# A fused two-layer block on one core: how each later stage begins, and who transposes x for it

## The chip, the core and the metric

One core of a Trainium2 chip runs the whole program in one launch. The time is the device time of one execution in microseconds; the median of three runs stands for the kernel. TensorE multiplies, VectorE and ScalarE prepare its operands and take its results away, GpSimd does a few small elementwise operations, and SyncE issues the weight loads.

## The reference, cut to what matters

x is 256 tokens by 2048 features, float32. Five stages follow one another, each a chain of large products with weights that are read once:

```
for layer in 0, 1:
    h = rms_norm(x, mix_pre_g[layer])
    m = pool_conformer_mixer(h, ...) if layer == 0 else short_conv_mixer(h, ...)
    x = x + rms_norm(m, mix_post_g[layer])
    h = rms_norm(x, ffn_pre_g[layer])
    x = x + rms_norm(relu(h @ w1) ** 2 @ w2, ffn_post_g[layer])
h = rms_norm(x, norm_g_2)
proj = h @ w_in          # q, k, v, z_a, u_b, v_b, z_b, g_a, g_b
x = x + (sigmoid(g_a) * y_a + sigmoid(g_b) * y_b) @ w_out
```

The stages are numbered 0 (mixer of layer 0), 1 (its feed-forward part), 2 (mixer of layer 1), 3 (its feed-forward part) and 4 (the last layer). Stages 1 to 4 are the "later stages": each needs all of the new x before it can multiply.

## The kernel before, in words

**Products.** Every float32 operand is split into a rounded part ("hi") and the rest ("lo"), and a product is three matmuls: lo times w_hi, hi times w_lo, hi times w_hi (`step_matmuls`, lines 835 to 837). A *chunk* is a product with 512 columns of weights; it is cut into *steps* of two 128-row tiles of weights. A step is 2 row tiles x 2 tiles of 128 tokens x 3 = 12 matmuls of 128x512. A chunk on x has 8 steps, and steps 0 and 1 need features 0 to 511 of x (its group 0), steps 2 and 3 group 1, steps 4 and 5 group 2, steps 6 and 7 group 3. The down chunks of the feed-forward stages have 4 steps. A chunk sums into two PSUM banks, `main_bank(c, tt)`, banks 0 to 3 by turns; banks 4 to 7 (`aux_bank`) take transposes.

**Who feeds a step.** SyncE loads the weights two steps at a time into three slots. ScalarE makes w_hi (line 800), VectorE makes w_lo (line 818). Both engines walk the same list of steps, `SEQ`; in the body of step s they have already split step s + 3 (`split_steps`, AHEAD = 3) and then do whatever other work is written for that step. A split has to wait until TensorE has finished the step six before it (SPLIT_SLOTS = 6). Each engine's order is written out by hand, so work in the body of step s stands ahead of the split for step s + 4.

**x for the next stage.** The stage multiplies by the transposed x, scaled by a gain for each feature; the row factor of the norm is applied when a chunk is taken from PSUM. At the end of a stage VectorE updates x group by group and tile by tile (`update`, line 1636). Each group then has to be transposed, scaled and split: *turned* by TensorE into PSUM (`turn`, line 886, or for one token tile `turn_tile`, line 903) or by VectorE in 32x32 blocks, 16 instructions for a group (`turn_last`, line 1554); then ScalarE makes the hi half (4 instructions) and VectorE the lo half (4 instructions). TensorE turns groups 0, 1 and 2, VectorE group 3 into `x_T`.

**The first steps of a later stage.** `boundary` lets TensorE finish the last four steps of the old stage for token tile 0, then for tile 1, then does the first four steps (HELD) of the new stage for tile 0, then for tile 1. Group 0 and 1 of tile 0 are turned before the last of the old steps, group 0 of tile 1 before the fourth of the new steps for tile 0, group 1 of tile 1 after the first new step for tile 1. `SEQ` opens a later stage with two chunks side by side: steps 0 to 3 of both, then steps 4 to 7 of both, so groups 0, 1, 2 and 3 are first needed at steps 0, 2, 8 and 10 of the opening. Group 2 is turned by TensorE after step 4. VectorE turns group 3 in the bodies of steps 3 to 6 (`early`), four blocks in each, and makes its lo half in that of step 7.

**Further work placed by step.** VectorE turns the squared hidden activations in the feed-forward stages (`turn_hidden`, eight steps for each, from `TURN_AT`), the gate parts in stage 2 and the queries and keys in stage 4 (`QK_TURNS`: first step after the chunk's end, and number of steps).

Of the kernel before, what the change touches and what calls it, by code (L numbers as in the profile page):

```python
# [41 lines left out]
TURN_STEPS = 8  # L42
STEP_K = 2
# [147 lines left out]
def pre_fills(p):  # L191

    return [("pre", p, g, tt, h) for tt in range(NT) for g in range(2) for h in range(2)] + \
           [("pre", p, g, h) for g in range(2, NG) for h in range(2)]
# [39 lines left out]
def small_banks():  # L234

    by_vector = {"h": range(2), "cu": range(NG), "bg": range(NG), "qk": range(4), "ws": range(2), "ao": range(2),
                 "zb": range(1, 2),
                 "merged": range(NG)}  # L240
    for key in turn_order():
        if key[0] == "pre" and key[1] > 0 and key[2] == NG - 1:
            continue
        if key[0] not in by_vector or key[1] not in by_vector[key[0]]:
            yield key
# [17 lines left out]
def build(nc, t):  # L263
    ctx = ExitStack()
    with ctx:
# [13 lines left out]

        LATE_PAIRS = (C_L2 + 30, C_L1 + 12,)  # L280
# [23 lines left out]

        TURN_AT = {}
        for layer in range(2):
            free = 0
            for b in range(NB):
                for j in range(2):
                    TURN_AT[layer, b, j] = max(free, S_END[up_chunk(layer, b, j)] + 1)  # L310
                    free = TURN_AT[layer, b, j] + TURN_STEPS + 1
# [59 lines left out]
        x_T = conv_out_flat[:, GK * TOK:2 * GK * TOK].rearrange("p (k t) -> p k t", k=GK)  # L371
# [101 lines left out]
        x_turned = signal("x_turned", [(p,) for p in range(1, 5)])  # L473
# [136 lines left out]

        def main_bank(c, tt):
            return bank[2 * (c % 2) + tt]
# [228 lines left out]
        def halves_key(c, i, tt):  # L841
# [5 lines left out]
            return key + ((tt, i % 2) if key[0] == "pre" and key[1] > 0 and g < 2 else (i % 2,))  # L847

        def wait_step(e, c, i, which):
# [6 lines left out]
            if i == 0 and c >= 2:  # L856
                for tt in which:
                    sem, value = taken(c - 2, tt)
                    e.wait_ge(sem, value)
# [11 lines left out]
        def pe_program(e):  # L871
# [17 lines left out]
            def turn_x(p, g, parts=two):  # L889
                if p == 0:  # L890
                    e.wait_ge(x_loaded[g], 16)
                else:
                    e.wait_ge(x_made.sem, x_made.of(p - 1, g, 1))
# [17 lines left out]
            def boundary(p):  # L911
# [8 lines left out]
                for i in range(HELD):  # L920
                    if i == HELD - 1:
                        turn_tile(p, 0, 1)
                    wait_step(e, f, i, (0,))
                    step_matmuls(e, f, i, (0,), None)
                for i in range(HELD):
                    if i == 1:
                        turn_tile(p, 1, 1)
                    wait_step(e, f, i, (1,))
                    step_matmuls(e, f, i, (1,), step_done)
# [96 lines left out]
            pe_mlp(e, turn_x, 0)  # L1026
# [3 lines left out]
            for c, i in matmul_steps(e, 2):  # L1030
                j, part = divmod(c - C_L1, 3)
                if (c, i) == (C_L1 + 1, 0):
                    turn_x(2, 2)

            boundary(3)
            pe_mlp(e, turn_x, 1)
# [3 lines left out]
            for c, i in matmul_steps(e, 4):  # L1040
                r = c - C_L2
                if (r, i) == (1, 0):
                    turn_x(4, 2)
# [46 lines left out]

        def pe_mlp(e, turn_x, layer):
            p = 1 + 2 * layer
            for c, i in matmul_steps(e, p):
                if (c, i) == (up_chunk(layer, 0, 1), 0):
                    turn_x(p, 2)
# [19 lines left out]
        def act_program(e):  # L1115
# [32 lines left out]
            def hi_turned(p):  # L1148

                e.wait_ge(x_turned.sem, x_turned.of(p))  # L1150
                for h in two:
                    for k in (2 * h, 2 * h + 1):
                        kt = GK * (NG - 1) + k
                        ins = e.activation(halves["A"][0][:, kt, :], x_T[:, k, :], ACT.Copy, scale=par_col(PRE_COL[p], kt))
                    ins.then_inc(hi_cast("pre", p, NG - 1, h), 1)
# [50 lines left out]
            def boundary(p):  # L1206
# [5 lines left out]
                hi_tile(p, 1, 0)  # L1212
# [3 lines left out]
                hi_tile(p, 1, 1)  # L1216
# [247 lines left out]
        def act_mlp(e, at, to_z, copy_acc, squares, early, layer):  # L1464
            p = 1 + 2 * layer
            for c, i in split_steps(e, p, split_hi, at):
# [12 lines left out]
                for b in range(NB):  # L1479
                    for j in two:  # L1480
                        if POS[c, i] == TURN_AT[layer, b, j] + TURN_STEPS:
# [41 lines left out]
        def dve_program(e):  # L1523
# [23 lines left out]
            def turn_last(p, n):  # L1547

                if n == 0:
                    e.wait_ge(x_made.sem, x_made.of(p - 1, NG - 1, 1))  # L1550
                tok = slice(32 * n, 32 * n + 32)
                for q in range(4):
                    feat = slice(32 * q, 32 * q + 32)
                    ins = e.transpose(x_T[feat, :, :].rearrange("p k (t c) -> p t k c", t=NT)[:, :, :, tok],
                                      x[tok, :, D - CH:].rearrange("p t (k c) -> p t k c", k=GK)[:, :, :, feat])
                if n == 3:
                    ins.then_inc(x_turned(p), 1)

            def lo_turned(p):

                hi, lo = halves["A"]
                for h in two:
                    e.wait_ge(hi_cast.sem, hi_cast.of("pre", p, NG - 1, h))
                    for k in (2 * h, 2 * h + 1):
                        kt = GK * (NG - 1) + k
                        ins = e.scalar_tensor_tensor(lo[:, kt, :], x_T[:, k, :], par_col(PRE_COL[p], kt),
                                                     hi[:, kt, :].bitcast(F32), ALU.mult, ALU.subtract)
                    ins.then_inc(lo_cast("pre", p, NG - 1, h), 1)
# [74 lines left out]
            def boundary(p, alone=False):  # L1643
# [7 lines left out]
                update(p - 1, 1, 0)  # L1651
# [4 lines left out]
                lo_part(p, 1, 0, 0)  # L1656
                settle(p - 1, 1)
                lo_part(p, 1, 0, 1)
# [6 lines left out]
                lo_tile(p, 1, 1)  # L1665
# [3 lines left out]
                split_to(e, split_lo, at, f + 5)  # L1669

            def early(p, c, i):
                if (c, i) == (STAGE[p] + 1, 0):
                    lo_x(p, 2)
                n = POS[c, i] - S0[STAGE[p]] - 3
                if 0 <= n < 4:
                    turn_last(p, n)
                if (c, i) == (STAGE[p] + 1, 3):
                    lo_turned(p)
# [51 lines left out]
            for c, i in split_steps(e, 2, split_lo, at):  # L1730
# [12 lines left out]
                if part == 2 and j < NG:  # L1743
                    if i == 0:
                        e.wait_ge(dve_took.sem, dve_took.of(c - 1, 1))
                        if j > 0:
                            e.wait_ge(short_made.sem, short_made.of(j - 1, SHORT_K - 1, GK - 1))
                    ins = turn_blocks(e, z[:, z_slot("c", j), :, :], short_in[:, :, SPAD:], i)
                    if i == TURN_STEPS - 1:
                        ins.then_inc(c_turned(j), 1)  # L1750
                for k in range(NG):
                    n = POS[c, i] - S0[C_L1 + 3 * k + 3] - (1 if k == NG - 1 else 0)
# [228 lines left out]
        def turn_hidden(e, layer, b, j, n):  # L1981
# [6 lines left out]
            ins = turn_blocks(e, z[:, z_slot("h", layer, b, j), :, :], h_T, n)  # L1988
            if n == TURN_STEPS - 1:
                ins.then_inc(turned(layer, b, j), 1)  # L1990

        def dve_mlp(e, at, finish_last, early, layer):
            p = 1 + 2 * layer
            for c, i in split_steps(e, p, split_lo, at):
# [13 lines left out]
                for b in range(NB):  # L2008
                    for j in two:
                        n = POS[c, i] - TURN_AT[layer, b, j]  # L2010
                        if 0 <= n < TURN_STEPS:
# [312 lines left out]
```

## Time and profile before

| | before |
|---|---|
| median of three runs | 2672.26 us (2672.09 to 2674.06) |
| the profiled execution: device time | 2672.57 us |
| its span, first to last instruction | 2670.8 us |
| TensorE busy | 2665.1 us, 100% |
| weight loads of TensorE busy | 2207.5 us, 83% |
| VectorE busy | 1960.8 us, 73% |
| ScalarE busy | 1289.0 us, 48% |
| GpSimd busy | 287.1 us, 11% |
| granted TensorE clock | 1.0 of full speed throughout |

A matmul's busy time in these views overlaps the next one's, because matmuls are pipelined: what one costs TensorE is the distance from its start to the next start. The device time is 1.8 us longer than the span; what is added to or taken from the span goes one to one into it.

### The profile page before, as it was taken

Reading aid. Unit: us, or ns where it says so; the run is one execution under the profiler, and the core shown is the slowest. Engines: PE = TensorE matmul, PEld = TensorE weight load, DVE = VectorE, ACT = ScalarE, POOL = GpSimd, SP = SyncE. Lnnn points to the kernel's source line nnn. Section 1 sums busy time; section 2 is a strip of 40 time slices with the busy share of each in tenths; the row PEclk is TensorE's granted clock in tenths of the full one; section 3 lists DMA queues with packets and bytes.
Section 4 is the critical chain, followed back from the end, with each engine's and each line's share of the span. In section 5 each row is a group of like instructions: output and inputs, shape, how many; then the busy total and the mean of one; then the engine's idle time right before and its main releaser. Section 6 shows DMA issues by size and latency. Waiting matters only on the chain.

```text
span 2670.8 us, 31092 instructions
## 1 busy us (share of the span) xinstructions
PE 2665.1 (100%) x11901; PEld 2207.5 (83%) x11901; DVE 1960.8 (73%) x2706; ACT 1289.0 (48%) x1625; POOL 287.1 (11%) x263
## 2 busy tenths in 40 slices
PE   9999999999999999999999999999999999999999
PEld 7888888888888888888888888888888888888887
DVE  6888867666766687777777676668668869985574
ACT  7775544444444454444544444344455545544452
POOL 5741100000000010000100000000011001000000
PEclk9999999999999999999999999999999999999999
DMA  8555655555655556555556655555555655565554
GB/s 263 183 174 195 210 194 189 189 189 191 207 186 190 202 185 210 192 199 193 189 191 204 204 189 184 195 189 194 190 184 188 210 176 174 175 217 191 189 204 143
DMA packets 268148, 515.57 MB, mean 193 GB/s; under 512 B 8498, under 2 KB 28260, under 8 KB 267492
## 3 DMA queue, kind: packets, MB, share of 16 engines
q1 hardware_dynamic: 267732, 513.34, 57.3%
q8 instruction: 97, 1.59, 0.2%
q14 instruction: 47, 0.39, 0.0%
q10 hardware_dynamic: 272, 0.26, 0.0%
HBM read 511.47 MB, written 2.10 MB: 192 GB/s over the span
## 4 chain that ended last, share of the span: by engine, by line
PE 99%; DVE 0%; DMA 0%; ACT 0%; issue 0%; SPq 0%; DVEq 0%; ACTq 0%
PE bank L835 32%; PE bank L837 32%; PE bank L836 32%; DMA w_raw<-in_ab_w_in 0%; PE bank L886 0%; PE bank L903 0%; PE bank L1087 0%; PE bank L971 0%; DVE w_lo L818 0%; PE bank L977 0%; PE bank L1101 0%; PE bank L968 0%; DVE tap_product L2116 0%; DVE z L2104 0%; PE bank L1073 0%; PE bank L1110 0%
## 5 line engine op out<-in xcount | busy, mean ns | idle before, releaser
L818 DVE TENSOR_TENSOR w_lo<-w_raw,w_hi 128x1024 fp32r<-128x1024 f32 x950 | 1182.6, 1264 | 438.0 <-ACT w_hi L800 431.4
L800 ACT ACTIVATE w_hi<-w_raw 128x1024 fp32r<-128x1024 f32 x954 | 972.8, 1056 | 614.8 <-PE bank L837 426.6
L835 PE MATMUL bank<-w_hi,A_lo 128*128 128x512 f32 x2408 | 941.0, 391 | 0.1
L837 PE MATMUL bank<-w_hi,A_hi 128*128 128x512 f32 x2408 | 937.8, 389 | 0.0
L836 PE MATMUL bank<-w_lo,A_hi 128*128 128x512 f32 x2408 | 937.6, 389 | 0.0
L835 PE MATMUL bank<-w_hi,B_lo 128*128 128x512 f32 x1408 | 548.9, 390 | 0.0
L837 PE MATMUL bank<-w_hi,B_hi 128*128 128x512 f32 x1408 | 548.1, 389 | 0.0
L836 PE MATMUL bank<-w_lo,B_hi 128*128 128x512 f32 x1408 | 548.0, 389 | 0.0
L835 PEld LDWEIGHTS bank<-w_hi,A_lo 128*128 128x128 f32 x2408 | 452.2, 188 | 95.1 <-issue 1.0
L837 PEld LDWEIGHTS bank<-w_hi,A_hi 128*128 128x128 f32 x2408 | 452.1, 188 | 94.3
L836 PEld LDWEIGHTS bank<-w_lo,A_hi 128*128 128x128 f32 x2408 | 452.2, 188 | 92.6
L837 PEld LDWEIGHTS bank<-w_hi,B_hi 128*128 128x128 f32 x1408 | 264.3, 188 | 55.0
L836 PEld LDWEIGHTS bank<-w_lo,B_hi 128*128 128x128 f32 x1408 | 264.4, 188 | 54.5
L835 PEld LDWEIGHTS bank<-w_hi,B_lo 128*128 128x128 f32 x1408 | 264.3, 188 | 54.5
L1977 DVE STREAM_TRANSPOSE conv_out<-z 32x256 f32<-32x256 f32 x512 | 223.1, 436 | 10.5
L1126 ACT ACTIVATE z<-bank,small 128x512 f32<-128x512 f32 x108 | 68.4, 686 | 326.8 <-PE bank L837 319.5
L2280 POOL TENSOR_TENSOR z<-z 128x512 f32<-128x512 f32 x64 | 65.2, 1040 | 1094.1 <-ACT z L1126 1094.1
L2004 DVE TENSOR_TENSOR acc<-bank,acc 128x512 f32<-128x512 f32 x96 | 61.8, 686 | 85.7 <-PE bank L837 85.7
L2161 POOL TENSOR_TENSOR acc<-acc,gain_row 128x512 f32<-128x512 f32 x32 | 40.9, 1296 | 518.6 <-ACT bank L1197 478.0
L1485 ACT ACTIVATE B_hi<-conv_out 128x512 fp32r<-128x512 f32 x64 | 37.1, 628 | 99.9 <-DVE conv_out L1977 99.9
L2155 POOL TENSOR_TENSOR small<-small,neg_half 128x1 f32<-128x1 f32 (+2 forms) x21 | 34.3, 1632 | 297.1 <-DVE small L1527 279.1
L1977 DVE STREAM_TRANSPOSE conv_in<-z 32x256 f32<-32x256 f32 x128 | 55.8, 436 | 2.6
(182 smaller groups left out, 1028.3 us busy)
## 6 DMA issues: line engine op xcount, KB each, us to landing
w_raw<-in_ffn_w SPq DMA_DIRECT2D x256, 1024.0 KB, 5.3
w_raw<-in_w_in SPq DMA_DIRECT2D x88, 1024.0 KB, 5.0
w_raw<-in_sc_w_in SPq DMA_DIRECT2D x48, 1024.0 KB, 5.1
w_raw<-in_ab_w_out SPq DMA_DIRECT2D x16, 1024.0 KB, 5.0
w_raw<-in_sc_w_out SPq DMA_DIRECT2D x16, 1024.0 KB, 5.0
w_raw<-in_w_out SPq DMA_DIRECT2D x16, 1024.0 KB, 5.0
w_raw<-in_ab_w_in SPq DMA_DIRECT2D x26, 512.0 KB, 5.0
w_raw<-in_ab_w_in SPq DMA_DIRECT2D x8, 1024.0 KB, 5.1
```

The lines of the kernel that those rows point to most:

```text
L800: e.activation(w_hi[:, s % SPLIT_SLOTS, :], raw_step(s), ACT.Copy).then_inc(hi_made, 1)
L818: e.tensor_tensor(w_lo[:, slot, :], raw_step(s), w_hi[:, slot, :].bitcast(F32), ALU.subtract).then_inc(lo_made, 1)
L835: e.matmul(ps, lo[:, kt, tok], wh, start=first, stop=False)
L836: e.matmul(ps, hi[:, kt, tok], wl, start=False, stop=False)
L837: ins = e.matmul(ps, hi[:, kt, tok], wh, start=False, stop=last)
L1126: e.activation(out(tt), main_bank(c, tt), func, scale=rs(layer_of(c))[:, tt:tt + 1]).then_inc(act_took(c, tt), 1)
L1485: e.activation(halves["B"][0][:, kt:kt + 2, :], h_T[:, 2 * h:2 * h + 2, :], ACT.Copy).then_inc(hi_cast("h", layer, b, j, h), 1)
L1977: ins = e.transpose(dst[feat, :, :].rearrange("p k (t c) -> p t k c", t=NT)[:, :, :, tok], src[tok, :, :].rearrange("p t (k c) -> p t k c" ...
L2004: e.tensor_tensor(out, main_bank(c, tt), out, ALU.add).then_inc(dve_took(c, tt), 1)
L2155: e.tensor_tensor(out, cols(n, "mean", *key), neg_half[:, 0:n], ALU.pow).then_inc(root_made(*key), 1)
L2161: e.tensor_tensor(out, out, gain_row[:, c], ALU.mult).then_inc(gained(p, n, tt), 1)
L2280: e.tensor_tensor(z[:, s, tt, :], z[:, s, tt, :], z[:, s, tt, :], ALU.mult).then_inc(squared(layer, b, j, tt), 1)
```

## The change

Every later stage opens with three chunks side by side on group 0 (steps 0 to 5), then on group 1 (6 to 11). Two of them go on with group 2 (12 to 15) and group 3 (16 to 19), and the third does its groups 2 and 3 in steps 20 to 23. The third chunk sums into the two transpose banks that held group 0 of tile 1. TensorE turns group 0 by tiles as before and group 1 whole, after the first four steps. VectorE turns group 2 in the bodies of steps 3 to 7 and group 3 in those of steps 8 to 12; the halves of group 2 are made in the body of step 9 and those of group 3 in the body of step 14. The first hidden turns take seven steps each, the first two down chunks of a feed-forward stage run side by side, and the turns of the queries and of stage 2 stand later.

```diff
+BY_VECTOR = (2, 3)
+X_TURNS = {2: (3, 5), 3: (8, 5)}
+X_HALVES = {2: 9, 3: 14}
-QK_TURNS = [(3, 6), (5, 6), (3, 5), (3, 5)]
+QK_TURNS = [(4, 6), (8, 6), (10, 6), (8, 6)]
-GATED_AT = [(C_L1 + 4, 3), (C_L1 + 7, 3), (C_L1 + 10, 3), (C_L1 + 13, 3)]
+GATED_AT = [(C_L1 + 4, 6), (C_L1 + 7, 3), (C_L1 + 10, 3), (C_L1 + 13, 3)]
...
             if first > 0:
                 for half in range(2):
-                    SEQ += [(c, 4 * half + i) for c in (first, first + 1) for i in range(4)]
-                rest = first + 2
+                    SEQ += [(first + n, 2 * half + i) for n in range(3) for i in range(2)]
+                for half in range(2, 4):
+                    SEQ += [(c, 2 * half + i) for c in (first, first + 1) for i in range(2)]
+                SEQ += [(first + 2, i) for i in range(4, 8)]
+                rest = first + 3
             while rest < end:
-                if rest in (6, 10):
+                if rest in (6, 10) or rest in FIRST_DOWN:
...
+        def hidden_steps(b):
+            return 7 if b == 0 else TURN_STEPS
...
+        THIRD = [STAGE[p] + 2 for p in range(1, 5)]
         def main_bank(c, tt):
+            if c in THIRD:
+                return aux_bank("pre", THIRD.index(c) + 1, 0, 1, tt)
             return bank[2 * (c % 2) + tt]
...
# TensorE, boundary
                     if i == n_steps[c] - 1:
                         turn_tile(p, 0, 0)
-                        turn_tile(p, 1, 0)
                     step_matmuls(e, c, i, (1,), step_done)
...
+                for n in range(HELD):
+                    if n == HELD - 1:
                         turn_tile(p, 0, 1)
+                    wait_step(e, *SEQ[S0[f] + n], (0,))
+                    step_matmuls(e, *SEQ[S0[f] + n], (0,), None)
+                for n in range(HELD):
+                    wait_step(e, *SEQ[S0[f] + n], (1,))
+                    step_matmuls(e, *SEQ[S0[f] + n], (1,), step_done)
+                e.wait_ge(x_made.sem, x_made.of(p - 1, 1, 1))
+                turn(lambda tt, part: x[:, tt, CH + part.start:CH + part.stop], "pre", p, 1)
...
-                if (c, i) == (up_chunk(layer, 0, 1), 0):
-                    turn_x(p, 2)
...
# ScalarE, early
-                if (c, i) == (STAGE[p] + 1, 0):
-                    hi_x(p, 2)
-                if (c, i) == (STAGE[p] + 1, 1):
+                n = POS[c, i] - S0[STAGE[p]]
+                if n == 5:
                     statistics(p)
-                if (c, i) == (STAGE[p], 4):
-                    hi_turned(p)
+                for g in BY_VECTOR:
+                    if n == X_HALVES[g]:
+                        hi_turned(p, g)
...
# VectorE, boundary: the new order
                 update(p - 1, 0, 0)
-                update(p - 1, 1, 0)
                 split_to(e, split_lo, at, f + 1)
                 lo_tile(p, 0, 0)
                 split_to(e, split_lo, at, f + 2)
                 finish(p - 1, NG - 1, 1, alone)
-                lo_part(p, 1, 0, 0)
+                update(p - 1, 1, 0)
                 settle(p - 1, 1)
-                lo_part(p, 1, 0, 1)
                 update(p - 1, 0, 1)
...
-                lo_tile(p, 1, 1)
                 split_to(e, split_lo, at, f + 4)
                 for tt in tiles:
                     update(p - 1, 3, tt)
                 split_to(e, split_lo, at, f + 5)
+                lo_x(p, 1)
 
             def early(p, c, i):
...
+                at_step = POS[c, i] - S0[STAGE[p]]
+                for g in BY_VECTOR:
+                    if at_step == X_HALVES[g]:
+                        lo_turned(p, g)
+                for g in BY_VECTOR:
+                    first, steps = X_TURNS[g]
+                    n = at_step - first
+                    if 0 <= n < steps:
+                        if n == 0:
+                            e.wait_ge(x_made.sem, x_made.of(p - 1, g, 1))
+                        ins = turn_blocks(e, x[:, :, g * CH:(g + 1) * CH], x_T[g], n, steps)
+                        if n == steps - 1:
+                            ins.then_inc(x_turned(p, g), 1)
                 if (c, i) == (STAGE[p], 4):
                     statistics(p)
```

## Rows read from the trace of the kernel before

**Rows 1.** The page, busy time of TensorE, and the chain that ended last.
```profile
PE 2665.1 (100%) x11901; PEld 2207.5 (83%) x11901; DVE 1960.8 (73%) x2706; ACT 1289.0 (48%) x1625; POOL 287.1 (11%) x263
...
PE 99%; DVE 0%; DMA 0%; ACT 0%; issue 0%; SPq 0%; DVEq 0%; ACTq 0%
```

**Rows 2.** Timeline of TensorE, opening of stage 1: start us, us, instruction, count.
```profile
243.35 1.04 PE L903 MATMUL bank<-ident,x_res 128*128 128x128 f32 x8
244.14 0.47 PE L835 MATMUL bank<-w_hi,B_lo 128*128 128x512 f32 x1
244.45 0.40 PE L836 MATMUL bank<-w_lo,B_hi 128*128 128x512 f32 x1
...
249.48 0.39 PE L837 MATMUL bank<-w_hi,A_hi 128*128 128x512 f32 x1
249.78 0.66 PE L903 MATMUL bank<-ident,x_res 128*128 128x128 f32 x4
...
253.23 0.60 PE L903 MATMUL bank<-ident,x_res 128*128 128x128 f32 x4
253.59 0.48 PE L835 MATMUL bank<-w_hi,A_lo 128*128 128x512 f32 x1
...
255.06 0.47 PE L835 MATMUL bank<-w_hi,A_lo 128*128 128x512 f32 x1
255.37 0.40 PE L836 MATMUL bank<-w_lo,A_hi 128*128 128x512 f32 x1
...
257.87 0.39 PE L835 MATMUL bank<-w_hi,A_lo 128*128 128x512 f32 x1
...
260.60 1.03 PE L886 MATMUL bank<-ident,x_res 128*128 128x128 f32 x8
```

**Rows 3.** Groups by line and shape, TensorE's transposes of x, whole run.
```profile
L903 PE MATMUL bank<-ident,x_res 128*128 128x128 f32 x64 | 9.2, 276 | 0.0
...
L886 PE MATMUL bank<-ident,x_res 128*128 128x128 f32 x56 | 7.6, 273 | 0.1
```

**Rows 4.** Waits, whole run: who waited for whom, us, times, longest.
```profile
PEld bank L903 <- DVE x_res L1636: 1.5, 4, 0.4
```

**Rows 5.** Timeline of VectorE, opening of stage 1.
```profile
248.15 0.16 DVE L1629 TENSOR_TENSOR small<-small 128x1 f32<-128x1 f32 x1 [0.34 <-ACT bank L1197]
...
248.97 0.75 DVE L1636 SCALAR_TENSOR_TENSOR x_res<-acc,small,x_res 128x512 f32<-128x512 f32 x1
...
257.81 1.22 DVE L818 TENSOR_TENSOR w_lo<-w_raw,w_hi 128x1024 fp32r<-128x1024 f32 x1
258.94 1.77 DVE L1554 STREAM_TRANSPOSE conv_out<-x_res 32x256 f32<-32x256 f32 x4
260.73 2.36 DVE L818 TENSOR_TENSOR w_lo<-w_raw,w_hi 128x1024 fp32r<-128x1024 f32 x2
263.01 1.66 DVE L1535 SCALAR_TENSOR_TENSOR A_lo<-bank,par,A_hi 128x256 fp32r<-128x256 f32 x4
...
266.49 1.22 DVE L818 TENSOR_TENSOR w_lo<-w_raw,w_hi 128x1024 fp32r<-128x1024 f32 x1
267.75 1.78 DVE L1554 STREAM_TRANSPOSE conv_out<-x_res 32x256 f32<-32x256 f32 x4
...
273.77 1.67 DVE L1566 SCALAR_TENSOR_TENSOR A_lo<-conv_out,par,A_hi 128x256 fp32r<-128x256 f32 x4
275.35 1.22 DVE L818 TENSOR_TENSOR w_lo<-w_raw,w_hi 128x1024 fp32r<-128x1024 f32 x1
...
276.56 3.49 DVE L818 TENSOR_TENSOR w_lo<-w_raw,w_hi 128x1024 fp32r<-128x1024 f32 x3
```

**Rows 6.** Timeline of ScalarE, hi halves of group 2.
```profile
261.23 0.47 ACT L1137 ACTIVATE A_hi<-bank,par 128x256 fp32r<-128x256 f32 x1 [4.54 <-PE bank L886]
261.60 0.47 ACT L1138 ACTIVATE A_hi<-bank,par 128x256 fp32r<-128x256 f32 x1
```

**Rows 7.** Timeline of GpSimd, the root for the stage's norm.
```profile
276.73 3.88 POOL L2155 TENSOR_TENSOR small<-small,neg_half 128x2 f32<-128x2 f32 x1 [21.34 <-DVE small L1527]
```

More of the change, by code:

```diff
@@ L191, in pre_fills @@
 def pre_fills(p):
-    return [("pre", p, g, tt, h) for tt in range(NT) for g in range(2) for h in range(2)] + \
-           [("pre", p, g, h) for g in range(2, NG) for h in range(2)]
+    return [("pre", p, 0, tt, h) for tt in range(NT) for h in range(2)] + \
+           [("pre", p, g, h) for g in range(1, NG) for h in range(2)]
 def turn_order():
@@ L241, in small_banks @@
     for key in turn_order():
-        if key[0] == "pre" and key[1] > 0 and key[2] == NG - 1:
+        if key[0] == "pre" and key[1] > 0 and key[2] in BY_VECTOR:
             continue
@@ L277, in build @@
         STAGE = (0, C_M0, C_L1, C_M1, C_L2, N_CHUNKS)
+        FIRST_DOWN = [down_chunk(layer, 0, 0) for layer in range(2)]
         LATE_PAIRS = (C_L2 + 30, C_L1 + 12,)
@@ L472, in build @@
                                    ([(g, tt) for tt in tiles for g in gs] if 0 in gs else [(g, tt) for g in gs for tt in tiles])])
-        x_turned = signal("x_turned", [(p,) for p in range(1, 5)])
+        x_turned = signal("x_turned", [(p, g) for p in range(1, 5) for g in BY_VECTOR])
         tap_done = signal("tap_done", DVE_TAPS)
@@ L846, in halves_key @@
                 return key + (i % 2, 0 if c == 0 else 1)
-            return key + ((tt, i % 2) if key[0] == "pre" and key[1] > 0 and g < 2 else (i % 2,))
+            return key + ((tt, i % 2) if key[0] == "pre" and key[1] > 0 and g < 1 else (i % 2,))
         def wait_step(e, c, i, which):
@@ L855, in wait_step @@
             e.wait_ge(lo_cast.sem, max(lo_cast.of(*halves_key(c, i, tt)) for tt in which))
[L856 to L859, printed above, removed]
+            if i == 0 and c in THIRD:
+                e.wait_ge(lo_cast.sem, lo_cast.of("pre", THIRD.index(c) + 1, 0, 1, 1))
+            elif i == 0 and c >= 2:
+                for before in (c - 4, c - 2) if c - 2 in THIRD else (c - 2,):
+                    for tt in which:
+                        sem, value = taken(before, tt)
+                        e.wait_ge(sem, value)
         def matmul_steps(e, stage):
@@ L889, in turn_x @@
             def turn_x(p, g, parts=two):
[L890 to L893, printed above, removed]
+                e.wait_ge(x_loaded[g], 16)
                 turn(lambda tt, f: x[:, tt, g * CH + f.start:g * CH + f.stop], "pre", p, g, parts=parts)
@@ L1025, in pe_program @@
             boundary(1)
-            pe_mlp(e, turn_x, 0)
+            for c, i in matmul_steps(e, 1):
+                pass
             boundary(2)
@@ L1031, in pe_program @@
                 j, part = divmod(c - C_L1, 3)
-                if (c, i) == (C_L1 + 1, 0):
-                    turn_x(2, 2)
             boundary(3)
-            pe_mlp(e, turn_x, 1)
+            for c, i in matmul_steps(e, 3):
+                pass
             boundary(4)
@@ L1480, in act_mlp @@
                     for j in two:
[L1481 removed]
+                        if POS[c, i] == TURN_AT[layer, b, j] + hidden_steps(b):
                             e.wait_ge(turned.sem, turned.of(layer, b, j))
@@ L1742, in dve_program @@
                 early(2, c, i)
[L1743 to L1750, printed above, removed]
+                for j in range(NG):
+                    made = C_L1 + 3 * j + 1
+                    n = POS[c, i] - S_END[made]
+                    if 0 <= n < TURN_STEPS:
+                        if n == 0:
+                            e.wait_ge(dve_took.sem, dve_took.of(made, 1))
+                            if j > 0:
+                                e.wait_ge(short_made.sem, short_made.of(j - 1, SHORT_K - 1, GK - 1))
+                        ins = turn_blocks(e, z[:, z_slot("c", j), :, :], short_in[:, :, SPAD:], n)
+                        if n == TURN_STEPS - 1:
+                            ins.then_inc(c_turned(j), 1)
                 for k in range(NG):
-                    n = POS[c, i] - S0[C_L1 + 3 * k + 3] - (1 if k == NG - 1 else 0)
+                    n = POS[c, i] - S0[C_L1 + 3 * k + 3] - (4 if k == 0 else 1 if k == NG - 1 else 0)
                     if 0 <= n < TURN_STEPS:
```

67 lines of the change are left out of this document (18 added, 49 removed).

## The prediction, made before the changed kernel had run

> **What bounds the kernel now.** I read the page first. TensorE is busy for 100% of the span and holds 99% of the chain that ended last [rows 1], so only two things can move the time: work taken from or given to TensorE, and pauses of TensorE that go away or appear. Then I read TensorE's timeline through the opening of stage 1. A step is 12 matmuls; step 4 begins at 257.87 and its last matmul is followed by the transposes at 260.60 [rows 2], so a step costs 2.72 us and one 128x512 matmul 0.227 us. The reader is to see in rows 2 that the engine is never idle for long, only that some starts are further apart than 0.227 us. Last I read VectorE's timeline at the same place, since it makes everything that the new order asks for, and the waits.
>
> **What TensorE saves.** Before, each of the four openings has 16 transposes by tiles (64 at line 903) and 8 for group 2 (32 of the 56 at line 886, the other 24 belonging to stage 0) [rows 3]. After, it has 4 + 4 for group 0 and 8 for group 1, so 8 transposes and one interruption go. Eight transposes hold TensorE for 244.14 - 243.35 = 0.79 us, and the gap behind the first matmul after them is 0.31 instead of 0.23 us, some 0.09 us more with what follows: 0.88 us for eight. Four of them cost 253.59 - 253.23 = 0.36, with the same tail 0.46 us [rows 2]. Four openings at 0.88 us would be 3.5 us, 0.13% of the time.
>
> **Where part of that is given back.** Group 1 of tile 0 leaves the place ahead of 243.35. That brings TensorE 0.42 us earlier to the transposes at 249.78, the ones of group 0, tile 1. But these waited for x already: the matmul before them is at 249.48, so without a wait they would stand at 249.71 [rows 2], and the waits list the same for all four openings [rows 4]. What they wait for is VectorE's update at 248.97, which ends at 249.72, and that one follows the small sum at 248.15, released by ScalarE's squares [rows 5]. The new order of VectorE only exchanges one update (0.67 us between starts) and two lo parts around this sum; the sum waits for ScalarE before and after, and I take that chain as unmoved. So the 0.42 us turn into waiting. Behind it the new opening saves the transposes at 253.23 (0.46 us), the pause of 0.08 us at 255.06 (its successor comes 0.31 us later instead of 0.23) and group 2's (0.88 us), and adds group 1's eight (0.88 us). Net gain by step 5 of the opening: 0.46 + 0.08 = 0.55 us, between 0.5 and, if VectorE's chain does get faster by its removed update, 0.95 us.
>
> **What VectorE has to do now.** It turns 32 blocks instead of 16 before the last of x is ready. Group 3 is needed at step 16, where step 10 was the point before. I count from the start of step 4, called 0 here, so that step 16 begins at 12 x 2.72 = 32.6 us. Prices, all [rows 5]: a block (260.73 - 258.94) / 4 = 0.4475 us; a split that is followed by a split or a half (263.01 - 260.73) / 2 = 1.14 us; a split that is followed by blocks 267.75 - 266.49 = 1.26 us, but 258.94 - 257.81 = 1.13 us ahead of a group's first block; four lo halves of a turned group 275.35 - 273.77 = 1.58 us.
>
> Start: group 1 is turned right ahead of step 4, in -0.88 to 0. ScalarE's first hi instruction came 0.63 us after the first transpose of group 2 (260.60 to 261.23), the second one ended at 261.60 + 0.47 [rows 2, 6]; some 0.06 us later, 1.53 us after the transposes' start, VectorE can begin the lo half. Its four instructions (0.42 us each, the second pair waiting for ScalarE's second pair until 2.37) end 3.2 us after that start, which is 2.3. VectorE has been free by then: before it reached this point at 258.94, one us behind 257.87, and now four lo instructions (1.04 us) fewer and none more stand ahead of it. So the queue starts at 2.3 whatever happened earlier.
>
> Then, by the written order: 3 blocks, splits 6 and 7, 3 blocks, split 8, 3, split 9, 3, split 10, 4 (group 2 turned at 15.7), split 11, 3, split 12, halves of group 2, 3, split 13, 3, split 14, 3, split 15, 4 (group 3 turned at 30.4), the statistics (0.07), splits 16 and 17, halves of group 3. Sum up to these halves: 32 x 0.4475 = 14.3; splits 4 x 1.14 (6, 12, 16, 17) + 7 x 1.26 (7, 8, 9, 10, 13, 14, 15) + 1.13 (11) = 14.5; 1.58; 0.07; with the start 2.3 this gives 32.8. TensorE is released by the first pair of halves, 0.39 + 0.47 + 0.06 = 0.92 us later: **33.7 against 32.6, so TensorE waits about 1.1 us at step 16**. On the way the other deadlines hold: split 6 is ready at 4.95 (step 6 at 5.44), group 2 at 20.2 (step 12 at 21.8), split 13 at 23.5 (24.5), splits 14 to 16 about 1 us early. The second pair of group 3 is ready at 34.5 and needed at 36.4. ScalarE is no part of it: its hi halves of group 3 start when the blocks end at 30.4 and are done by 32.2, ahead of VectorE.
>
> The same count on the kernel before: from 258.94, 16 blocks, five splits and four lo halves bring the halves of group 3 to 273.8, as the row at 273.77 has it, ready for TensorE at 274.7, and step 10 began at 257.87 + 6 x 2.72 + 0.88 = 275.1. The margin was 0.4 us. The change adds 16 blocks (7.2 us), seven splits (8.6 us) and a start 1.2 us later against step 4, 16.9 us with the statistics, and moves the deadline by six steps less the 0.88 us of group 2's transposes, 15.4 us: 1.1 us late from this side too.
>
> Unseen forms: three blocks at a time and reading group 2 of x in place of group 3. The neighbouring forms bound a block by 0.438 and 0.452 us (the 2-block pieces of the hidden turns), -0.3 to +0.15 us in all. A split could save 0.12 us seven times if it never met the longer gap: -0.9 us. So the wait at step 16 lies between 0 and 1.4 us; I take 1.1, since each price is that of the same instruction with the same neighbours.
>
> **Edits taken at nothing.** The third chunk sums in other PSUM banks: same matmuls, and nothing else fills those banks until the next opening. Seven-step hidden turns: two or three blocks beside a split are at most 1.26 + 1.34 = 2.6 us in a 2.72 us step. The second hidden half is now cast in the body of step 34 for step 36 instead of 30 for 34; the body of step 34 begins for VectorE while TensorE is in step 33, the cast takes under 3 us, and I see 2 us of cover left. If that were gone, two stages would pay. Statistics on VectorE at step 12 instead of 8: the root is wanted at step 18 instead of 12. The gain row's load stands one weight load earlier in SyncE's queue; the multiply that releases it needs the update of x's group 2, which comes about 4 us before the next weight load could be issued. Query turns: later, less crowded, and still ahead of the attention's first scores.
>
> **The sum.** 4 x (1.08 - 0.55) = +2.1 us on the profiled 2672.57, so 2674.7; against the median 2672.26 it is **2674.3**, +0.08%. A difference below 0.2% (5.3 us) is about what a measurement of this kernel cannot tell from none.
>
> **What pages say against it.** The Trainium skill, "VectorE: DVE Perf Modes", "Rules for kernel authors", advises TensorE for a 128x128 transpose when PSUM will do, and its section on the three paths gives 390 ns for one on TensorE; by that figure 32 removed transposes would be worth 12.5 us. The trace has 0.11 us for one in a row of eight, so the measurement decides. The same page's section on the TRN2 errata gives 58 cycles plus one for each element at 0.96 GHz: 327 ns for a block by estimate, where the row has 447; by it 32 blocks would take 3.8 us less and step 16 would not wait.
>
> **Rivals.** *Group 3 is in time* (0.30): VectorE's queue is 1.1 us shorter than I count. For it: the gap ahead of blocks has two sizes (1.13 and 1.26), and the margin before was as thin as 0.4 us without a pause. Against it: 0.9 us is all that this can give. Then only the gain is left: -4 x 0.55 = -2.2 us, 2670.1; with the other end of the gain at the boundary, -3.6, 2668.7.
> *GpSimd holds the last splits off* (0.13): its root now falls on splits 16 and 17, which are on the path. It takes 3.88 us [rows 7]; if a split had to wait for it, step 16 would come up to 3.9 us later in each opening, +2.1 + 15.6 us, 2690; it decides against "no change" from 0.8 us an opening on. Against it: before, the root at 276.73 ran beside three splits that took 3.49 us together, the usual pace [rows 5, 7]. I keep the chance mainly for a small slip of this size, because with no slack left each us on VectorE costs four.
> *The forecast* (0.57): 2671.5 to 2676.5.
>
> **Numbers.** The range reaches from 2669.5 (the first rival) to 2677.5 (a wait of 1.9 us). Faster by over 0.2% is beyond the whole saving of 3.5 us plus the pauses at the boundaries (about 1 us): 0.03. Slower by over 0.2%: most of the second rival, 0.12. Within: 0.85.
>
> **What would show it.** The whole-group line still has 56 transposes of x (group 1 in place of group 2), the by-tile line 32 instead of 64. TensorE waits about 0.5 us, up from 0.07, at the transposes of group 0, tile 1. At step 16 of each opening, about 33 us after step 4, a gap of 1.1 us waits for VectorE's lo halves of group 3, and VectorE is busy without a pause from 2.3 to 34 us. I am wrong if there is no such gap, if it stands at another step, or if the transposes of group 0, tile 1 come 0.4 us earlier than I say.

## The result, and the profile after

| | before | after |
|---|---|---|
| median of 22 runs | 2672.62 us (2672.09 to 2674.06) | 2677.05 us (2676.55 to 2678.87) |
| the profiled execution, its span | 2672.57, 2670.8 us | 2676.63, 2674.9 us |
| TensorE busy | 2665.1 us | 2662.8 us |
| VectorE busy | 1960.8 us | 1992.7 us |

The changed kernel takes 1.0017 times the time of the one before (95% interval 1.0011 to 1.0022): 4.4 us more. That is inside the 0.2% that I called "no change", on the slower side as forecast, and twice the size of the forecast (+2.1 us). The range, up to 2677.5 us, holds it by 0.45 us only, and the narrower band of the forecast (2671.5 to 2676.5) does not. With 22 runs of each the interval is clear of 1.

The page's busy times, as [rows 1]: TensorE lost 32 transposes, VectorE won 48 instructions (64 blocks more, 16 lo parts fewer, since group 1 is no longer made by tiles). By line and shape, 56 transposes of x stand in the whole-group form and 32 in the by-tile form, as forecast.

```profile
PE 2662.8 (100%) x11869; PEld 2204.8 (82%) x11869; DVE 1992.7 (74%) x2754; ACT 1285.8 (48%) x1609; POOL 281.3 (11%) x263
```

TensorE's timeline at the two places that matter in the opening of stage 1, as [rows 2] (start us, us, instruction, idle before it and who ended it).

```profile
242.96 0.60 PE L918 MATMUL bank<-ident,x_res 128*128 128x128 f32 x4
243.31 0.48 PE L850 MATMUL bank<-w_hi,B_lo 128*128 128x512 f32 x1
...
248.69 0.39 PE L852 MATMUL bank<-w_hi,A_hi 128*128 128x512 f32 x1
249.76 0.66 PE L918 MATMUL bank<-ident,x_res 128*128 128x128 f32 x4 [0.68 <-DVE x_res L1629]
...
257.29 1.03 PE L904 MATMUL bank<-ident,x_res 128*128 128x128 f32 x8
258.08 0.48 PE L850 MATMUL bank<-w_hi,A_lo 128*128 128x512 f32 x1
...
290.59 0.39 PE L852 MATMUL bank<-w_hi,A_hi 128*128 128x512 f32 x1
292.06 0.47 PE L850 MATMUL bank<-w_hi,A_lo 128*128 128x512 f32 x1 [1.08 <-DVE A_lo L1559]
```

Two gaps stand there that were not there, or hardly, before. From the matmul at 248.69 to the transposes of group 0, tile 1 it is 1.07 us, where the kernel before has 0.30 and 0.23 would be no wait; and step 16 of the opening begins 1.47 us after the last matmul of step 15. All four openings show them in the same size: 1.03 to 1.07 and 1.46 to 1.48 us. The waits list has the two, and [rows 4] with 1.5 us in all is the only one of them that was there before.

```profile
PEld bank L850 <- DVE w_lo L833: 6.4, 5, 1.5
PEld bank L918 <- DVE x_res L1629: 4.4, 4, 1.1
PE bank L850 <- DVE A_lo L1559: 4.3, 4, 1.1
```

The first of these lines is largely the pause of step 16 once more, seen by the weight loads: the load that follows it stands at 292.03, after 1.48 us, and the list puts that wait down to a split. The split of step 16 had ended at 289.99 (288.77 + 1.22), two microseconds before; the halves had not.

Matched matmul by matmul, the changed kernel falls behind by 1.10, 1.14, 1.13 and 1.0 us in its four openings and by nothing behind or between them (in the first 80 us, before any opening, its profiled execution happens to be 0.4 us ahead): the third chunk's banks, the side-by-side down chunks, the seven-step hidden turns and the later query turns cost nothing that can be seen.

VectorE's timeline of that opening, as [rows 5].

```profile
242.12 1.22 DVE L833 TENSOR_TENSOR w_lo<-w_raw,w_hi 128x1024 fp32r<-128x1024 f32 x1
244.04 1.13 DVE L1569 SCALAR_TENSOR_TENSOR A_lo<-bank,par,A_hi 128x128 fp32r<-128x128 f32 x4 [0.70 <-ACT A_hi L1170]
...
246.81 1.40 DVE L1629 SCALAR_TENSOR_TENSOR x_res<-acc,small,x_res 128x512 f32<-128x512 f32 x1
248.14 0.15 DVE L1622 TENSOR_TENSOR small<-small 128x1 f32<-128x1 f32 x1
248.95 0.75 DVE L1629 SCALAR_TENSOR_TENSOR x_res<-acc,small,x_res 128x512 f32<-128x512 f32 x1 [0.66 <-POOL small L2155]
...
253.92 1.22 DVE L833 TENSOR_TENSOR w_lo<-w_raw,w_hi 128x1024 fp32r<-128x1024 f32 x1
255.05 2.45 DVE L1629 SCALAR_TENSOR_TENSOR x_res<-acc,small,x_res 128x512 f32<-128x512 f32 x2
...
258.80 1.66 DVE L1540 SCALAR_TENSOR_TENSOR A_lo<-bank,par,A_hi 128x256 fp32r<-128x256 f32 x4 [0.16 <-ACT A_hi L1144]
260.37 1.32 DVE L1977 STREAM_TRANSPOSE conv_out<-x_res 32x256 f32<-32x256 f32 x3
...
286.87 1.79 DVE L1977 STREAM_TRANSPOSE conv_out<-x_res 32x256 f32<-32x256 f32 x4
288.69 0.17 DVE L1532 TENSOR_SCALAR small<-small 128x2 f32<-128x2 f32 x1
288.77 2.35 DVE L833 TENSOR_TENSOR w_lo<-w_raw,w_hi 128x1024 fp32r<-128x1024 f32 x2
291.04 1.67 DVE L1559 SCALAR_TENSOR_TENSOR A_lo<-conv_out,par,A_hi 128x256 fp32r<-128x256 f32 x4
```

From 258.80 to 291.04 the engine has no pause at all, and TensorE starts 1.02 us after the halves begin. ScalarE does not hold them: its hi halves of group 3 run from 288.69 for 1.71 us and end 0.64 us before VectorE's begin. VectorE's idle time ahead of the halves of group 1 is 0.16 us: the cover that I had counted on without measuring it. And one update of x, at 246.81, takes 1.40 us where the next one takes 0.75; two more, at 255.05, take 2.45 us where the kernel before has 1.41. What ran beside them is in GpSimd's timeline (with the root of the norm, which answers to [rows 7]):

```profile
246.37 1.29 POOL L2161 TENSOR_TENSOR acc<-acc,gain_row 128x512 f32<-128x512 f32 x1 [4.96 <-DVE w_lo L833]
248.37 0.55 POOL L2155 TENSOR_TENSOR small<-small,neg_half 128x1 f32<-128x1 f32 x1 [0.70 <-DVE small L1622]
254.08 2.21 POOL L2161 TENSOR_TENSOR acc<-acc,gain_row 128x512 f32<-128x512 f32 x1 [5.17 <-DVE x_res L1629]
288.94 1.61 POOL L2155 TENSOR_TENSOR small<-small,neg_half 128x2 f32<-128x2 f32 x1 [32.65 <-DVE small L1532]
```

In the kernel before, the same two multiplies took 1.30 and 1.29 us, and what VectorE did beside them, a sum and lo parts with one large input in PSUM, took its usual 0.68 and 0.34 us. GpSimd's timeline of it, and one row of VectorE's:

```profile
246.76 1.30 POOL L2161 TENSOR_TENSOR acc<-acc,gain_row 128x512 f32<-128x512 f32 x1 [4.92 <-DVE w_lo L818]
254.10 1.29 POOL L2161 TENSOR_TENSOR acc<-acc,gain_row 128x512 f32<-128x512 f32 x1 [5.17 <-DVE x_res L1636]
...
256.48 1.41 DVE L1636 SCALAR_TENSOR_TENSOR x_res<-acc,small,x_res 128x512 f32<-128x512 f32 x2
```

### The profile page after: what moved, and what is told of

Its sections match the earlier page's. It is cut to its first block, busy times and chain, and to the rows that moved or that the text cites. A ratio compares the mean times of both kernels' runs of the same rounds, so it can differ in the third digit from the quotient of the medians.

```text
span 2674.9 us, 31048 instructions
## 1 busy us (share of the span) xinstructions
PE 2662.8 (100%) x11869; PEld 2204.8 (82%) x11869; DVE 1992.7 (74%) x2754; ACT 1285.8 (48%) x1609; POOL 281.3 (11%) x263
## 4 chain that ended last, share of the span: by engine, by line
PE 93%; DVE 6%; ACT 1%; issue 1%; POOL 0%; DVEq 0%; POOLq 0%; ACTq 0%
PE bank L850 30%; PE bank L852 30%; PE bank L851 30%; DVE w_lo L833 2%; DVE conv_out L1977 2%; DVE A_lo L1559 0%; ACT w_hi L815 0%; PE bank L904 0%; PE bank L1099 0%; DVE A_lo L1540 0%; PE bank L982 0%; PE bank L985 0%; PE bank L991 0%; POOL acc L2161 0%; PE bank L952 0%
## 5 line engine op out<-in xcount | busy, mean ns | idle before, releaser
L2155 POOL TENSOR_TENSOR small<-small,neg_half 128x1 f32<-128x1 f32 (+2 forms) x21 | 25.2, 1201 | 331.1 <-DVE small L1532 311.5
```

The costliest lines, as they stand in the source:

```text
L2155: e.tensor_tensor(out, cols(n, "mean", *key), neg_half[:, 0:n], ALU.pow).then_inc(root_made(*key), 1)
```

## The experiments

Theory: step 16 waits for the end of a full VectorE queue (1.24 us), and the transposes of group 0, tile 1 wait 0.84 us, of which GpSimd's multiply causes 0.35 us by holding off one of VectorE's updates. Rivals: ScalarE or the weights hold step 16; the update is slow by itself; the new order costs by itself. Every kernel below is the changed one with the edit shown, timed against the kernel before on the same chip (2672.6 to 2672.8 us); the gaps are read start to start in the four openings of one execution, 0.23 us being none. The medians are of 11 executions each, 22 for the changed kernel and 5 for the full dose.

| kernel | gap at group 0, tile 1 | gap at step 16 | median us | ratio to before, 95% |
|---|---|---|---|---|
| changed | 1.03 to 1.07 | 1.46 to 1.48 | 2677.05 | 1.0017 (1.0011 to 1.0022) |
| update of group 1 later | 0.65 to 0.70 | 1.81 to 1.87 | 2677.07 | 1.0016 (1.0007 to 1.0025) |
| multiply later | 0.65 to 0.69 | 1.45 to 1.48 | 2675.72 | 1.0012 (1.0003 to 1.0020) |
| halves in step 13 | 1.03 to 1.06 | 0.30 to 0.35 | 2672.62 | 1.0000 (0.9991 to 1.0008) |
| update later, halves in 13 | 0.67 to 0.68 | 0.69 to 0.74 | 2672.44 | 0.9999 (0.9990 to 1.0008) |
| 12 blocks of group 2 left out | 1.06 to 1.07 | none | 2671.70 | 0.9997 (0.9988 to 1.0005) |
| multiply later, halves in 13 | 0.69 to 0.70 | 0.32 to 0.35 | 2671.04 | 0.9994 (0.9985 to 1.0003) |
| the same, wait filled | none | 0.63 to 0.68 | 2670.57 | 0.9992 (0.9983 to 1.0001) |
| half dose | 1.04 to 1.07 | 1.91 to 1.94 | 2678.91 | 1.0024 (1.0015 to 1.0033) |
| full dose | 1.05 to 1.07 | 2.30 to 2.34 | 2686.99 | 1.0053 (1.0040 to 1.0065) |
| multiply later, halves in 13, full dose | 0.67 to 0.70 | 1.16 to 1.20 | 2674.40 | 1.0006 (0.9998 to 1.0015) |

**The halves of group 3 one step earlier.**

```diff
-X_HALVES = {2: 9, 3: 14}
+X_HALVES = {2: 9, 3: 13}
```

> The halves of group 3 are made in the body of step 13 instead of 14, so one split (1.14 us) stands behind them and no longer ahead. Theory (step 16 waits for the end of a full VectorE queue): the gap of 1.47 us at step 16 falls to about 0.35, 4 x 1.1 = 4.4 us less: about 2672.6. Rival (TensorE is held there by ScalarE's hi halves or by weights): the gap stays, 2677. Second rival (the split for step 17, pushed back by 1.6 us, becomes late): the gap moves to step 17 and less than 2 us are won.

2672.62 us; the gap at step 16 is gone but for 0.1 us. One split fewer ahead of the halves is worth 4.4 us. The split for step 17 now comes some 1.5 us later against TensorE and is still in time. The edit also moves ScalarE's hi halves ahead of one of its own splits, so the time alone does not acquit ScalarE; the rows do. Against the last matmul of step 15 its halves begin 1.90 us early in the changed kernel (288.69, 290.59) and 1.92 us here (289.55, 291.47), whenever the blocks are done, while VectorE's come 1.16 us sooner (0.45 us after that matmul there, 0.71 us before it here). The split of step 16 and its weights stand where they stood. The timelines of ScalarE, VectorE and TensorE at step 16:

```profile
289.55 1.72 ACT L1160 ACTIVATE A_hi<-conv_out,par 128x256 fp32r<-128x256 f32 x4 [7.55 <-DVE conv_out L1977]
290.76 1.67 DVE L1559 SCALAR_TENSOR_TENSOR A_lo<-conv_out,par,A_hi 128x256 fp32r<-128x256 f32 x4
...
291.47 0.39 PE L852 MATMUL bank<-w_hi,A_hi 128*128 128x512 f32 x1
291.78 0.47 PE L850 MATMUL bank<-w_hi,A_lo 128*128 128x512 f32 x1
```

**Twelve of group 2's blocks left out.**

```diff
+                        if g == 2 and n < steps - 1:
+                            continue
                         ins = turn_blocks(e, x[:, :, g * CH:(g + 1) * CH], x_T[g], n, steps)
```

> The changed kernel without 12 of VectorE's 16 transposes of group 2 (x's group 2 is then not turned, the output is not the reference's): 5.4 us less work on VectorE in each opening. Theory: no gap at step 16, 4 x 1.24 = 5.0 us less: 2672.1; what is left of the change then costs nothing against the kernel before, since the saving of 0.9 us at the transposes is given back to 0.8 us by the wait at group 0, tile 1. Rival (the new order of the steps or the third chunk's banks cost by themselves): above 2674.

2671.70 us: 5.3 us less, no gap at step 16. The kernel does not compute the reference's output; it only weighs VectorE's queue. Twelve of the 16 blocks moved to VectorE are more than that wait, and the new order of steps, free of it, costs nothing that can be seen.

**The update of group 1, tile 0 later in VectorE's order.**

```diff
...  (x_made is counted in the new order)
-                update(p - 1, 1, 0)
                 settle(p - 1, 1)
                 update(p - 1, 0, 1)
                 split_to(e, split_lo, at, f + 3)
                 lo_tile(p, 0, 1)
+                update(p - 1, 1, 0)
                 update(p - 1, 1, 1)
```

> VectorE's update of group 1, tile 0 goes behind the halves of group 0, tile 1 (and x_made is counted in that order). In the changed kernel this update took 1.40 us beside GpSimd's gain multiply, against 0.75 for a lone one, and pushed the small sum to 248.14. Theory (the update is held by GpSimd and delays the chain that TensorE waits for at the transposes of group 0, tile 1): the sum comes 0.3 us earlier, the gap of 1.07 us there falls to about 0.72, four openings give 1.4 us back: about 2675.7. Rival (that chain is set by ScalarE's squares alone, so the update sits in a pause): no change of the gap, 2677.1.

2677.07 us: the time that the rival gave, and the rival was still wrong. The first gap fell by 0.37 us as the theory had it; the one at step 16 grew by 0.38 (1.47 to 1.85) and ate it. VectorE's timeline shows how:

```profile
258.12 1.22 DVE L833 TENSOR_TENSOR w_lo<-w_raw,w_hi 128x1024 fp32r<-128x1024 f32 x1
259.26 1.65 DVE L1540 SCALAR_TENSOR_TENSOR A_lo<-bank,par,A_hi 128x256 fp32r<-128x256 f32 x4
260.83 1.32 DVE L1977 STREAM_TRANSPOSE conv_out<-x_res 32x256 f32<-32x256 f32 x3
```

TensorE turned group 1 at 257.32 there, against 257.29 in the changed kernel, but the blocks begin at 260.83 instead of 260.37: the update, moved behind the pause, used up the 0.16 us of idle time ahead of group 1's halves and 0.4 us more. Only the time hid that; the two gaps told it. GpSimd's second multiply had taken the rest of the cover: the two updates beside it take 2.45 us here too. With the 1.41 us of the kernel before, 1.04 us less, the cover would be about 1.2 us and would swallow the moved update. That is an estimate from these rows; no kernel here moves the second multiply.

**GpSimd's multiply later, VectorE's order untouched.**

```diff
-                e.wait_ge(lo_made, S0[STAGE[p + 1]] + 3)
-                gain(p, NG - 1, 0)
                 root(1, "postroot", "post", p, 1)
+                e.wait_ge(lo_made, S0[STAGE[p + 1]] + 4)
+                gain(p, NG - 1, 0)
```

> VectorE's order stays that of the changed kernel; GpSimd makes the second root before its gain multiply for the last 512 columns of tile 0, and that multiply waits for one split more. Theory (the two engines hold each other off): VectorE's update of group 1, tile 0 falls from 1.40 to about 0.75 us, the gap at the transposes of group 0, tile 1 from 1.07 to about 0.72, four openings -1.4 us: 2675.7, as with the other order. Rival (the update is slow for a reason of its own, as the semaphore of the gain): it stays at 1.4 us and so does the time.

2675.72 us, 1.3 less, and no change at step 16. VectorE's timeline: the same update, now with GpSimd idle beside it, takes 0.74 us, so it was not slow by itself, and the small sum waits for ScalarE again, as it did before the change.

```profile
247.24 0.74 DVE L1629 SCALAR_TENSOR_TENSOR x_res<-acc,small,x_res 128x512 f32<-128x512 f32 x1
248.18 0.16 DVE L1622 TENSOR_TENSOR small<-small 128x1 f32<-128x1 f32 x1 [0.20 <-ACT bank L1203]
```

**Edits together.** The first two kernels are sums of edits above.

> Both edits. If they are independent, the gains add: -1.4 - 4.4 us, about 2671.3, 0.05% below the kernel before. If VectorE's later update eats into the time ahead of step 16, less: the update only moves within the boundary, ahead of a pause, so I expect none of that.

> GpSimd's multiply moved and group 3's halves in the body of step 13. Theory: both gains add, since moving the multiply left the gap at step 16 as it was (1.45 to 1.48 us): 2677.05 - 1.4 - 4.4 = 2671.2, 0.05% below the kernel before. Rival (as with the other order of the update, the time comes back at step 16): 2672.4.

The first came to 2672.44 us, not 2671.3: the later update again costs at step 16 what it gives ahead of it (0.74 against 0.35 us). The second came to 2671.04, the two gains in full. In the last of these kernels TensorE turns group 1's tile 0 in the remaining wait; `turn_part(p, 1, tt)` makes the four transposes of one token tile (its definition is left out here):

```diff
                     if n == HELD - 1:
+                        turn_part(p, 1, 0)
                         turn_tile(p, 0, 1)
...
-                e.wait_ge(x_made.sem, x_made.of(p - 1, 1, 1))
-                turn(lambda tt, part: x[:, tt, CH + part.start:CH + part.stop], "pre", p, 1)
+                turn_part(p, 1, 1)
```

> The same with group 1's tile 0 turned by TensorE in the wait ahead of group 0, tile 1 (0.69 us from start to start, 0.46 of it waiting). Theory: the wait is filled, and the four transposes are missing after step 3: 0.42 us an opening; part comes back at step 16, because VectorE's queue starts at a fixed point after group 1's halves and TensorE arrives sooner: 0.2 to 0.3 us. Net 4 x 0.15 = 0.6 us less: 2670.6. Rival (TensorE's gain is kept in full): 2669.5; rival (the filled wait delays the transposes of group 0, tile 1): 2671.5 or more.

2670.57 us, 0.08% below the kernel before (interval 0.9983 to 1.0001, so only just short of certain). Eight transposes run where there was a wait:

```profile
249.32 0.39 PE L852 MATMUL bank<-w_hi,A_hi 128*128 128x512 f32 x1
249.55 0.60 PE L927 MATMUL bank<-ident,x_res 128*128 128x128 f32 x4
250.01 0.66 PE L918 MATMUL bank<-ident,x_res 128*128 128x128 f32 x4
```

and the gap at step 16 rises from 0.35 to about 0.65 us, since TensorE gets there sooner and VectorE does not.

**Doses.** A useless sum on VectorE in the body of step 10 (the "full dose") measures the slack directly.

```diff
+                        if g == 3 and n == 2:
+                            e.tensor_tensor(scores_flat, x[:, 0, 0:768], x[:, 0, 768:1536], ALU.add)
```

> The changed kernel with one useless VectorE instruction more in the body of step 10 of each opening: a sum of two 128x768 pieces of x into a free buffer (the result is not touched), about 0.95 us. Theory (VectorE has no slack from group 1's halves to group 3's): the gap at step 16 grows by what the instruction takes, from 1.47 to about 2.4 us, 4 x 0.95 = 3.8 us more: 2680.9. Rival (some of VectorE's time there is covered): the gap grows by less than half of it, under 2679.

The gap grew as the theory says: the instruction stands 0.96 us in the queue, the split ahead of it is followed 0.11 us sooner, and the gap went from 1.47 to 2.32 us, +0.85. But the time rose by 9.9 us, not by 3.4 (3.8 by the expectation). TensorE's timeline behind step 16, and then its granted clock in four stretches (us; busy time and count of TensorE, weight loads, VectorE, ScalarE and GpSimd; clock; DMA share and GB/s):

```profile
291.71 0.39 PE L852 MATMUL bank<-w_hi,A_hi 128*128 128x512 f32 x1
294.03 0.47 PE L850 MATMUL bank<-w_hi,A_lo 128*128 128x512 f32 x1 [1.93 <-DVE A_lo L1559]
...
295.60 0.63 PE L850 MATMUL bank<-w_hi,A_lo 128*128 128x512 f32 x1
296.02 0.63 PE L851 MATMUL bank<-w_lo,A_hi 128*128 128x512 f32 x1
```

```profile
291.00:294.00 3.00, 1.10 (x5) 0.56 (x4) 3.00 (x5) 3.00 (x6) 1.52 (x1) 1.00 0.69 253
294.00:295.50 1.50, 1.47 (x6) 1.29 (x7) 1.50 (x3) 1.22 (x2) 0.00 (x0) 0.94 0.85 186
295.50:298.50 3.00, 3.00 (x8) 2.31 (x8) 2.58 (x3) 0.00 (x0) 0.00 (x0) 0.50 0.83 304
298.50:302.00 3.50, 3.50 (x16) 2.82 (x15) 0.00 (x0) 0.52 (x1) 0.00 (x0) 0.97 0.74 259
```

From 295.5 to 298.5 the clock is at 0.50, the lower level of 1.2 GHz, and matmuls start 0.43 us apart instead of 0.23. Seven starts at that distance, and the slower ones at either end, add 1.6 us, in each of the four openings: 4 x (0.85 + 1.6) = 9.8 us. Over the whole execution the clock is 0.997 or 0.998 in all five runs of this kernel, and 1.000 in every run of the others. Two more kernels tell the clock from the instruction: one with half the columns (the "half dose", its line below), and one with the full dose in the kernel with the multiply later and the halves in step 13.

```diff
+                            e.tensor_tensor(scores_flat[:, 0:384], x[:, 0, 0:384], x[:, 0, 768:1152], ALU.add)
```

> As the dose before, with half the columns (384): about 0.55 us, 0.45 net, because the split ahead of it is then followed 0.11 us sooner. With the full dose the gap at step 16 grew by 0.85 us (1.47 to 2.32), as the theory had it, but 1.2 us later TensorE ran some three us at the lower of its two clocks, 1.6 us more for each opening, and the time was 9.9 us up instead of 3.8. Theory A (the clock falls only behind the longer pause): gap about 1.9 us, no slow stretch: 2677.05 + 1.8 = 2678.9. Theory B (any added pause brings it on): a slow stretch in each opening, 2685.

> The full dose (768 columns, 0.85 us net) in the kernel with GpSimd's multiply moved and group 3's halves in step 13 (2671.0). Theory (the dose costs its own length while the pause stays short): the gap at step 16 goes from 0.35 to about 1.2 us, no stretch at the lower clock, 4 x 0.85 = 3.4 us: 2674.4. Rival (the useless instruction itself disturbs, whatever the pause, by reading x beside others): 9.9 us more as in the changed kernel, 2681.

2678.91 and 2674.40 us, both as the dose's own length says. The half dose gave a gap of 1.93 us and no slow stretch. The full dose, in a kernel where the gap ends at 1.2 us, cost 3.4 us. So the instruction does not cost more than its length by itself. What fell behind the pause of 2.3 us, and behind neither of the shorter ones, is the clock.

## Why the prediction was right, and where it was too small

- **What TensorE saves**: as forecast. Four transposes leave 0.35 us between starts (242.96 to 243.31), 32 transposes are gone, and the by-tile ones stand where they should.
- **The wait ahead of group 0, tile 1**: forecast as 0.42 us more than before, measured 0.77 in this opening (a wait of 0.84 us, before 0.07). The failed step is "the sum waits for ScalarE before and after, and I take that chain as unmoved". I had priced the update moved there at 0.67 us and saw that it fits ahead of the sum; I had not asked what else uses its place. GpSimd's multiply runs there, and the update took 1.40 us. The kernel with the multiply moved gave that part back: 0.37 us an opening, 1.3 us in all.
- **The GpSimd rival**: refuted, two splits in 2.35 us beside the root at 288.94. Its price was also misread. The 3.88 us of [rows 7] are not the root's own length: without VectorE work beside it a root of this shape takes 0.71 us in the same trace, and the 3.88 us ended 0.56 us after the third of the splits beside it (276.56 + 3.49 = 280.05, against 280.61). In the changed kernel it takes 1.61 us and ends 0.56 us after the first split. GpSimd was the one that waited; no run shows this root holding off a split, and 3.9 us at step 16 had no ground in the rows. Its row, from stage 0 of the kernel before:

```profile
32.09 0.71 POOL L2155 TENSOR_TENSOR small<-small,neg_half 128x2 f32<-128x2 f32 x1 [13.50 <-DVE small L1527]
```

- **Step 16**: the mechanism and the place were right, 1.08 us forecast, 1.24 measured. From the start of the blocks at 260.37 to the halves at 291.04 it is 30.67 us, where my count has 30.5. The difference is in seams that I took from other neighbours: the split behind four blocks comes 1.82 us after them, not 1.79, and blocks behind halves 1.69 us after these, not 1.58. Two more terms were off by 0.1 us each and cancel: TensorE follows the halves after 1.02 us instead of 0.92, and step 16 is due 32.74 us after step 4 (290.59 + 0.23 - 258.08) instead of 32.64.
- **The start of the queue** ("it starts at 2.3 whatever happened earlier"): true for the changed kernel, but by 0.16 us. With updates as short as in the kernel before it would have been 1.2 us, by estimate; GpSimd's second multiply took the rest (255.05). The kernel with the later update crossed that line.
- **The edits taken at nothing**: all held; no matmul outside the openings moved against the kernel before, and with 12 blocks left out the kernel is at 2671.7.
- **The sum**: 4 x (1.24 + 0.35 - 0.55) = 4.2 us; measured 4.4. The forecast of +2.1 lacks 0.35 us of the multiply and 0.16 of the seams, four times. The rest is about the 0.08 us by which the second matmul of step 16 comes late (292.06 to 292.37, 0.31 instead of 0.23 us).
- **The Trainium skill's prices**: the Trainium skill, "VectorE: DVE Perf Modes", "The three transpose paths", has its 390 ns for a bf16 transpose, which the prediction does not say; the float32 ones here leave TensorE as little as the row said, 0.35 us for four. The blocks took 0.45 us again, so the estimate of 327 ns does not hold either. The advice of its "Rules for kernel authors" to keep 128x128 transposes on TensorE fits the first result: moving them to a full VectorE queue cost 4.4 us. With one split out of the way the two are even (2672.62 us).

## What to carry to other kernels

Work taken off the bounding engine is worth its length only if the receiving queue has slack to its next deadline: add up that queue's instructions from the last point at which it is known to be idle, with the seams between kinds, and compare with the deadline in the bounding engine's steps. Where the sum is late by less than one movable instruction, change the order before giving up the edit: here one split put behind the last halves was worth 4.4 us. And when an edit moves an instruction into a pause, look at which other engine works in it, and read that engine's durations with and without company before you call one its price.

## What the runs showed of the hardware that I had not expected

- VectorE and GpSimd hold each other off when both stream large tensors from SBUF. A 128x512 update with two of its inputs there took 1.40 us beside GpSimd's 128x512 multiply and 0.74 us without it. GpSimd's second multiply, begun 0.16 us after a VectorE split, took 2.21 us instead of 1.29, and the update behind that split was late in turn. The Trainium skill, "SBUF — State Buffer", "SBUF: two separate sides", says that a VectorE operation with two SBUF inputs and a GpSimd one that reads SBUF take one pair of ports in turn, each for a whole instruction. The trace agrees in the main: each time the later one ends only after the earlier one. It does not show a full instruction behind that end: the updates end 0.54 us after the multiply (247.67 and 248.21; 256.29 and 256.83) where one alone takes 0.74. VectorE's lo parts, with one large input in PSUM, ran beside the same multiply at 0.34 us each, and the multiply took its 1.30 us.
- GpSimd's root on 128x2 is held too, though it is tiny: 0.71 us alone, 1.61 and 3.88 us beside VectorE's splits, ending 0.56 us after one of them each time. The splits beside it kept their pace. Why it got in behind the first split in one kernel and only behind the third in the other is not shown.
- A pause of TensorE of 2.3 us, start to start, was followed 1.2 us after its end by a little over 3 us at half the clock, four times out of four; pauses of 1.91 to 1.94 us and shorter ones never were (four openings each in ten kernels). So a change that lengthens such a pause from 1.9 to 2.3 us can lose 1.6 us more than the wait explains; what happens between the two was not measured.
- A VectorE transpose of 32 partitions by 256 costs 0.45 us in a row, and a split is followed by it after 1.26 us instead of 1.14 unless it is the first block of a group (1.14 too).
